# A hybrid layer: prompt attention, delta stages, memory keys and sample attention put together anew

## The reference, cut to what matters

```python
def gdn_chunked(q, k, v, g, beta, s0):          # per chunk of c rows and head
    gcum = cumsum(g)
    dec_strict, dec_incl = exp(gcum_i - gcum_j) for i > j, i >= j
    tmat = eye(c) + beta * dec_strict * (k @ k.T)
    w  = solve(tmat, beta * exp(gcum) * k)      # unit lower triangular
    uv = solve(tmat, beta * v)
    qk = (q @ k.T) * dec_incl
    u  = uv - w @ s
    o  = exp(gcum) * (q @ s) + qk @ u
    s  = exp(gcum_last) * s + (k * exp(gcum_last - gcum)).T @ u

def mem_kv(mem, g_mem, w_xk, w_xv, g_xk):
    mn = rmsnorm(mem, g_mem)
    return rmsnorm((mn @ w_xk) by heads, g_xk), mn @ w_xv
```

## Time and profile before

| | |
|---|---|
| median of three runs | 3438.41 us |
| profiled execution | 3432.61 us, span 3430.7 us |
| mean granted TensorE clock | 0.944 |
| prompt attention | 742.5 to 1129.1 us of the span |
| gate stage | 1129.1 to 1150.3 |
| prompt delta stage | 1150.3 to 1545.4 |
| sample delta stage | 1545.4 to 1653.8 |
| window attention of the sample | 1653.8 to 1771.0 |
| memory keys | 1771.0 to 1831.5 |
| output projection | from 1831.5 |

### The profile page before, as it was taken

One profiled execution on the slowest core, in us unless ns is written; L12 is line 12 of the kernel. 1 busy time (PEld: TensorE's weight loads), 2 busy tenths in 40 slices (PEclk: granted clock), 3 DMA queues, 4 the chain that ended last, 5 costly groups with the idle time before them and its releaser, 6 DMA issues. The chain is left out here.

```text
span 3430.7 us, 63305 instructions
## 1 busy us (share of the span) xinstructions
PE 3035.9 (88%) x22904; PEld 2636.5 (77%) x22949; DVE 1782.0 (52%) x2700; ACT 1472.6 (43%) x2924; POOL 411.2 (12%) x394
## 2 busy tenths in 40 slices
PE   7999999979999599975557999599749999999998
PEld 7999999978888488864335888488638888888886
DVE  5244055545554355553324776244377867676572
ACT  5112145435556365542122332255425655565552
POOL 1000000000000000000320000111112222222222
PEclk9999999989999799996688999799869999999999
DMA  5333433223335211111772433533349988989792
GB/s 170 115 107 129 162 110 116 92 86 124 123 127 170 75 36 57 64 47 45 241 245 81 137 126 111 183 115 136 124 168 325 323 291 295 330 300 320 227 316 55
DMA packets 299855, 549.18 MB, mean 160 GB/s; under 512 B 80675, under 2 KB 136879, under 8 KB 299130
## 3 DMA queue, kind: packets, MB, share of 16 engines
q1 hardware_dynamic: 261722, 406.68, 35.1%
q0 software_dynamic: 33712, 137.63, 12.8%
q10 hardware_dynamic: 4224, 2.10, 0.2%
HBM read 436.49 MB, written 143.39 MB: 169 GB/s over the span
## 5 line engine op out<-in xcount | busy, mean ns | idle before, releaser
L136 PE MATMUL pj_pu<-pj_w,pj_nT 128*128 128x256 f32 (+3 forms) x1088 | 307.2, 282 | 0.0
L137 PE MATMUL pj_pu<-pj_w,pj_nT 128*128 128x256 f32 (+3 forms) x1088 | 306.3, 282 | 0.0
L138 PE MATMUL pj_pu<-pj_w,pj_nT 128*128 128x256 f32 (+3 forms) x1088 | 305.6, 281 | 0.0
L137 PEld LDWEIGHTS pj_pu<-pj_w,pj_nT 128*128 128x128 f32 (+1 forms) x1088 | 202.5, 186 | 0.0
L138 PEld LDWEIGHTS pj_pu<-pj_w,pj_nT 128*128 128x128 f32 (+1 forms) x1088 | 202.4, 186 | 0.0
L136 PEld LDWEIGHTS pj_pu<-pj_w,pj_nT 128*128 128x128 f32 (+1 forms) x1088 | 202.0, 186 | 0.1
L3183 ACT ACTIVATE ex_gate<-xw_gate_raw 128x2048 fp32r<-128x2048 f32 x64 | 120.7, 1918 | 167.8 <-PE ex_gu L138 96.5
L716 ACT ACTIVATE att_prob<-att_score,att_res 128x256 f32<-128x256 f32 (+1 forms) x384 | 127.6, 443 | 142.6 <-DVE att_res L752 142.6
L3244 DVE TENSOR_TENSOR ex_down<-xw_down_raw,ex_down 128x2048 fp32r<-128x2048 f32 x64 | 146.6, 2291 | 79.7 <-ACT ex_down L3183 62.3
L136 PE MATMUL pj_pu<-pj_nT,pj_w 128*128 128x384 f32 (+2 forms) x480 | 175.3, 365 | 0.0
L758 DVE COPY att_pT<-att_turn 128x512 f32<-128x512 f32 (+1 forms) x192 | 107.3, 573 | 129.3 <-PE att_turn L812 128.8
(11 more groups left out here) (581 smaller groups left out, 7877.0 us busy)
## 6 DMA issues: line engine op xcount, KB each, us to landing
xw_gate_raw<-in_w_gate SPq DMA_DIRECT2D x64, 1024.0 KB, 6.9
xw_up_raw<-in_w_up SPq DMA_DIRECT2D x64, 1024.0 KB, 9.2
xw_down_raw<-in_w_down SPq DMA_DIRECT2D x64, 1024.0 KB, 11.2
out_win_k<-in_cache_k POOLq DMA_DIRECT2D x8, 2032.0 KB, 13.0
out_win_v<-in_cache_v POOLq DMA_DIRECT2D x8, 2032.0 KB, 13.7
tmp_att<-att_res POOLq DMA_DIRECT2D x48, 264.0 KB, 4.6
po_att<-tmp_att SPq DMA_DIRECT2D x16, 792.0 KB, 4.5
pj_raw<-in_w_in SPq DMA_DIRECT2D x24, 512.0 KB, 5.4
```

Of the source, the lines that this page charges most:

```text
L136: pe.matmul(out, ah, bh, start=start, stop=False)
L137: pe.matmul(out, ah, bl, start=False, stop=False)
L138: return pe.matmul(out, al, bh, start=False, stop=stop)
```

## The change

Prompt attention and prompt delta stage are put into one stage, "ag", which holds the attention's result ring, the gate inputs, six of the delta constants (the seventh, ident, comes with the gate inputs) and the ring of input tiles. SP issues the loads of all these behind its last attention load. POOL's wait for the attention stores moves to the end of delta_prompt's POOL program. The gate block has no SP program any more; the rows are stored and read back at the start of delta_prompt's main block, and PE waits for them only before the first tile's sums. As before, each DMA adds 16 to its semaphore.

The sample delta stage is a new function, delta_sample, in one block and with 64 rows (`C` = 64) throughout. The state's loads, four of 512 KB, z and one gain are issued on ACT's queue ahead of its first exponential. The state now is the weight (128x128), and 16 columns, eight rows of the turned W and of q of that sequence (`WQ`), move through it; the result is turned back by PE. The masked u is made by ACT, the eight products for the new state go through four banks, and the state is stored by SP in four pieces, two after each half. The memory rows, gains and the two weights for the memory keys are loaded by SP during this block.

memory_kv now follows at once, and during it SP loads queries, keys and values of the first sequence for the window attention, which comes next. The first rows for project_out lie in the tile `raw` of the weight split, and are loaded in the window attention's block, after POOL's splits are done and ahead of the stores of its results.

The diff, cut to its core (`-` lines of the old sample stage are left out):

```diff
+    with Stage(nc, "ag") as o:
+        res = o.sb("res", [P, 4, AH * (AD + 1) + AH])
...
+        def first_inputs(sp):
+            for dst, src in ((ab[:], t["zab"][0:PT, :, BW:].rearrange("n p c -> p n c")), (par[:], t["gate_par"]),
+                             (ss[:].rearrange("p a h n -> p (a h n)"), t["ss"]), (m[:], t["gp_sums"]), (ident[:], t["ident"])):
+                sp.dma_start(dst, src).then_inc(sems["loaded"], 16)
+            for dst, name in ((identb, "identb"), (eye, "gp_eye"), (sel, "gp_sel"), (maskb, "gp_mask"), (lvl, "gp_lvl"), (gout, "g_gdn")):
+                sp.dma_start(dst[:], t[name]).then_inc(sems["consts_in"], 16)
+            for n in range(3):
+                sp.dma_start(uu[:, n].rearrange("p a h d -> p (a h d)"), t["uu"][n]).then_inc(sems[f"u_in{n}"], 16)
+
+        attend_prompt(nc, t, res, att_stored, first_inputs)
+        delta_prompt(nc, t, (ab, ss, par, m, piece, ident), (identb, eye, sel, maskb, lvl, gout, uu), sems, att_stored)
...
+                ahead(sp)
...
-                for k in range(RES):
-                    pool.wait_ge(stored[k], NB // RES * 16)
...
+                sp.dma_start(ab[:].rearrange("p a h -> p (a h)"), t["zab"][PT, R, BW:]).then_inc(E["gates_in"], 16)
+                sp.dma_start(par[:], t["gate_par"][R]).then_inc(E["gates_in"], 16)
+                sp.dma_start(m[:], t["gs_sums"][R, :, R]).then_inc(E["gates_in"], 16)
+                sp.dma_start(uu[:].rearrange("p a h d -> p (a h d)"), t["uu"][PT, R]).then_inc(E["u_in"], 16)
+                for dst, name in ((ident, "ident"), (rm, "gs_rows"), (ones, "ones"), (identb, "identb"), (maskb, "gs_mask"), (lvl, "gs_lvl")):
+                    sp.dma_start(dst[:], t[name]).then_inc(E["consts_in"], 16)
+                if ahead:
+                    ahead(sp)
+                sp.wait_ge(E["pad_ok"], 1)
+                sp.wait_ge(E["ob_ok"], 1)
+                sp.dma_start(t["ob"][PT], ob[:].rearrange("p h d -> p (h d)")).then_inc(E["stored"], 16)
+                for a in range(2):
+                    sp.wait_ge(E["S_ok"], BH * a + BH)
+                    for b in (4 * a, 4 * a + 2):
+                        sp.dma_start(t["delta_s"][b:b + 2].rearrange("b h k v -> k (b h) v"),
+                                     S[:, b:b + 2].rearrange("p b h d -> p (b h) d")).then_inc(E["S_out"], 16)
+                sp.wait_ge(E["stored"], 16)
+                sp.wait_ge(E["S_out"], 64)
...
+                act.dma_start(z[:].rearrange("p h d -> p (h d)"), t["zab"][PT, R, 0:BW]).then_inc(E["z_in"], 16)
+                act.dma_start(gout[:], t["g_gdn"]).then_inc(E["z_in"], 16)
+                for b in range(0, B, 2):
+                    act.dma_start(S[:, b:b + 2].rearrange("p b h d -> p (b h) d"), t["delta0"][b:b + 2].rearrange("b h k v -> k (b h) v")).then_inc(E["S_in"], 16)
+                act.wait_ge(E["gates_in"], 48)
+                act.activation(na[:], par[:, 0], ACT.Exp).then_inc(E["na_ok"], 1)
+                act.wait_ge(E["ax_ok"], 1)
+                act.activation(ax[:], ax[:], ACT.Exp).then_inc(E["ln_ok"], 1)
...
+                for b in range(B):
+                    if b == 4:
+                        act.wait_ge(E["o_mm"], 1)
+                        act.activation(sqo[:], po, ACT.Square).then_inc(E["o_sq"], 1)
+                    act.activation(um[:, b], u[:], ACT.Copy, scale=rm[R, 0, b:b + 1]).then_inc(E["um_ok"], 1)
...
+                def decayed(b):
+                    V(S[:, b], S[:, b], bc(last[:, :, b], [P, BH, BD]), ALU.mult).then_inc(E["Sl_ok"], 1)
+
+                def grown_by(n):
+                    a, h = divmod(n, BH)
+                    dve.wait_ge(E["Sl_ok"], 4 * a + 4)
+                    dve.wait_ge(E["ds_mm"], n + 1)
+                    V(S[:, 4 * a:4 * a + 4, h, :], S[:, 4 * a:4 * a + 4, h, :], grown[n % 4], ALU.add).then_inc(E["S_ok"], 1)
...
+                pe.wait_ge(E["S_in"], 64)
+                pe.wait_ge(E["qgT_ok"], 1)
+                pe.wait_ge(E["WT_ok"], 1)
+                flat = pt[:].rearrange("p a h n -> p (a h n)").rearrange("p (h b k) -> p h b k", h=BH, b=B)
+                for h in range(BH):
+                    for b in range(B):
+                        mm = pe.matmul(flat[:, h, b, :], S[:, b, h, :], WQ[:, h, :, DEC_T * b:DEC_T * b + DEC_T], start=True, stop=True)
+                mm.then_inc(E["wq_mm"], 1)
...
+                for n in range(2 * BH):
+                    a, h = divmod(n, BH)
+                    pe.wait_ge(E["um_ok"], 4 * a + 4)
+                    need(pe, E["S_ok"], n - 3)
+                    pe.matmul(grown[n % 4], kt[:, h], um[:, 4 * a:4 * a + 4, h, :], start=True, stop=True).then_inc(E["ds_mm"], 1)
...
-            @block.sync
-            def _(sp):
-                for dst, src in ((ab[:], t["zab"][0:PT, :, BW:].rearrange("n p c -> p n c")), (par[:], t["gate_par"]),
-                                 (ss[:].rearrange("p a h n -> p (a h n)"), t["ss"]), (m[:], t["gp_sums"]), (ident[:], t["ident"])):
-                    sp.dma_start(dst, src).then_inc(loaded, 16)
-                sp.wait_ge(dv, 25)
-                sp.dma_start(t["b_rows"].rearrange("k p m t -> m (k p) t"), piece[:].rearrange("m k p t -> m (k p) t")).then_inc(kept, 16)
-                sp.wait_ge(kept, 16)
-                sp.dma_start(rw[:], t["b_rows"].rearrange("k p (h n) t -> (p h) k n t", h=BH)).then_inc(rows_in, 16)
-                sp.wait_ge(rows_in, 16)
...
-                rows(0)
-                for dst, name in ((ident, "ident"), (identb, "identb"), (eye, "gp_eye"), (sel, "gp_sel"), (maskb, "gp_mask"), (lvl, "gp_lvl"), (gout, "g_gdn")):
-                    sp.dma_start(dst[:], t[name]).then_inc(E["consts_in"], 16)
-                for n in range(1, PT):
+                sp.dma_start(t["b_rows"].rearrange("k p m t -> m (k p) t"), piece[:].rearrange("m k p t -> m (k p) t")).then_inc(E["kept"], 16)
+                sp.wait_ge(E["kept"], 16)
+                sp.dma_start(rw[:], t["b_rows"].rearrange("k p (h n) t -> (p h) k n t", h=BH)).then_inc(E["rows_in"], 16)
+                for n in range(3, PT):
...
+                for done in att_stored:
+                    pool.wait_ge(done, 12 * 16)
...
+                    if n == 0:
+                        pe.wait_ge(E["rows_in"], 16)
...
+                    if b or not first:
+                        values(b)
...
+        def first_sequence(sp):
+            sp.dma_start(q[0:NS], t["q"][PT, 0:NS]).then_inc(keyed["q_in"], 16)
+            for dst, cache, new, near, far in ((kk[:, 0], t["cache_k"][0], t["k"], "k_near0", "k_far0"), (vv[:, 0], t["cache_v"][0], t["v"], "v_in0", "v_in0")):
+                sp.dma_start(dst[:, 2:6, :], cache[W_BUF // 2:].rearrange("(j p) c -> p j c", p=P)).then_inc(keyed[near], 16)
+                sp.dma_start(dst[0:DEC_T, 6, :], new[PT, 0:DEC_T]).then_inc(keyed[near], 16)
+                for j in range(2):
+                    rows = cache[0:W_BUF // 2].rearrange("(j n r) c -> j n r c", j=2, r=16)[j, :, 0:DEC_T, :]
+                    sp.dma_start(dst[:, j, :], rows).then_inc(keyed[far], 16)
...
+            def mem_inputs(sp):
+                sp.dma_start(ident[:], t["ident"]).then_inc(keyed["consts_in"], 16)
+                for dst, src in ((x[:], t["mem"].rearrange("n p d -> p n d")), (gm[:], t["g_mem"]), (gk[:], t["g_xk"])):
+                    sp.dma_start(dst, src).then_inc(mem_in["loaded"], 16)
+                for n, name in enumerate(("w_xk", "w_xv")):
+                    sp.dma_start(w[:, n], t[name].rearrange("(k p) c -> p k c", p=P)).then_inc(mem_in["w_in"], 16)
+
+            delta_sample(nc, t, mem_inputs)
+            memory_kv(nc, t, (ident, x, w, gm, gk), mem_in, keyed["consts_in"], first_sequence)
...
+            att = raw[:, 0:3 * WA].rearrange("p (a n) -> p a n", a=3)
+            cat = raw[:, 3 * WA:3 * WA + D]
+            gq = raw[:, 3 * WA + D:3 * WA + D + XD]
+            eye = raw[:, 3 * WA + D + XD:3 * WA + D + XD + P]
...
+                sp.wait_ge(raw_free, len(loads))
+                for dst, name in ((eye, "ident"), (gq, "g_xq")):
+                    sp.dma_start(dst, t[name]).then_inc(consts_in, 16)
+                sp.dma_start(att, t["att"][:, 0].rearrange("a p c -> p a c")).then_inc(att_in, 16)
                 sp.dma_start(cat[:, AW:], t["ob"][0]).then_inc(ob_in, 16)
 
-            memory_kv(nc, t, first_rows)
-            project_out(nc, t, w, wq, (ident, gq, att, cat), sems)
+            attend_sample(nc, t, False, lambda pool, s: halves_ahead(pool, s, loads, (gx[:], t["g_xattn"]), raw_free), first_rows, (ident, q, kk, vv, keyed))
+            project_out(nc, t, w, wq, (eye, gq, att, cat), sems)
```

More of the change, by code:

```diff
@@ L651, in attend_prompt @@
         raw_in = s.sem("raw_in0", "raw_in1", "raw_in2")
-        stored = s.sem(*[f"stored{k}" for k in range(RES)])
         v_in = s.sem("v_in0", "v_in1", "v_in2", "v_in3")
@@ L1047, in delta_net @@
-        G = gates(nc, s, t, cst, tiles, first, 0 if sample else 2, pk, constants)
```

(38 more changed lines are left out.)

810 lines of the change are left out of this document (293 added, 517 removed).

## The result

The changed kernel takes 3379.07 us (median; 3378.79 to 3384.86) against 3438.41: a ratio of 0.9824, interval 0.9810 to 0.9837. It was forecast at 3357, and falls into the range; of the 81 us forecast, 59 came.

A forecast was written before the change was run, and what follows sets the result against it. PE, busy 88% of the span, loses time where it stands still, mostly in chains of waits. Terms 7.2+11.0-0.7+45+11.2+7+0.7 = 81.4 us off 3432.6 give 3351.2, as a median 3357; range 3337 to 3382.

The forecast's parts named there:

- rival A: Sample delta stage stays slow, PE at low clock and ACT issues at 1.35: gain 30 not 45, 3372 us; chance 0.22.
- rival B: Window stage gives nothing, DMA at 0.91 and added loads eating what is saved: 3364 us; chance 0.12.
- Part 1: End of prompt attention to gates: store wait removed, gate loads issued early, so DVE starts 7.2 us earlier.
- Part 2: Gates to first sums: constants and input tiles already loaded, only exit, store and reload left; 11.0 us less.
- Part 3: The stage holding the shared tiles has its own exit: 0.7 us more.
- Part 4: Sample delta stage, cut at five points: 108.4 us becomes 63.2, 45 us less.
- (a): Sample delta stage, start to transposes of the keys: one block, inputs loaded beside the gates; 22.7 to 17.0 us.
- (c): Sample delta stage, solve's first matmul to products with the state: half widths, two masked DVE copies gone; 13.8 to 6.9 us.
- (d): Sample delta stage, state products to first products for the new state: 64 weight loads at 8.3; 23.6 to 13.7 us.
- (e): Sample delta stage, new-state products to last addition's end: four banks, masks on ACT, PE and DVE overlap; 24.0 to 12.8 us.
- (f): Sample delta stage's tail: half the state stored early, two stores remain; 11.5 to 6.3 us.
- Part 6: Window attention: first sequence already loaded, second key load goes out earlier, fewer bytes; 7 us less, ends 0 and 12.

The follow-up runs named there:

- second profile: Changed kernel run again with no edit and profiled: median 3375.13 us, profile span 3373.8 us.
- first profile: Profile of the changed kernel as first measured, of its slowest execution: 3384.86 us, span 3383.2 us.

## Why the prediction was right, and where it was not

The direction, the order of the parts and the range held; the sum was 22 us too large by the medians. Half of that is one term. The range held because its slow end was set by rival A's time, plus 10: A and B, which the prediction priced one at a time, came together, and their 15 and 7 us make 3379. That this is the median to the microsecond is luck, since parts 1 to 3 and 5 fell short by 1 to 5 us each as well.

- **Part 4**, cut by cut, forecast and then measured (second profile): (a) 17.0, 16.3; (b) 6.5, 5.9; (c) 6.9, 11.5; (d) 13.7, 19.1; (e) 12.8, 14.8; (f) 6.3, 8.1. What failed in (d) is the clock: I took the state products at 8.3, near the full clock's 6.9, and they took 13.83, above the low-clock bound of 12.5 that I had worked out; that is the whole excess of (d), and with the clock up 36 of the 64 went at 0.103 each. Rows of the old stage speak for such a price, but for a reason that the change removes. Its two sets of state products (windows, columns as above):

```profile
1594.70:1603.30 8.60, 8.57 (x64) 8.60 (x65) 2.08 (x1) 0.00 (x0) 0.00 (x0) 0.80 0.00 0
1603.30:1610.50 7.20, 7.20 (x68) 7.03 (x66) 0.68 (x1) 0.00 (x0) 0.00 (x0) 1.00 0.01 2
```

  They had a PEclk of 0.80 and 1.00. But that clock had come up in the old stage's own work ahead of them, and the rewrite puts products half as wide in its place; the new stage is at 0.50 from its start to its end. No run separates what in the new work leaves the clock low. For (c) and (e) the low clock is argued: PE is busy for 9.0 of 11.6 us in (c) and nearly throughout (e), all at 0.50, and no run has either with the clock up. Estimate for (c): with these 9.0 halved it would take 7.1, near the forecast's 6.9. Rival A named this cause and the gain that it leaves, 30; measured 33. Its other half came too: the six issues on ACT took 8.0 us in the first profile and not 4.8, but only 3.5 to 4.4 of them lay on the path, so (a) held. What failed in (f) is the queue: I had half of the state stored early, but in SP's program these stores stand behind the wait for the output rows, and all four went out together. One sum was also wrong: the extremes named for (a), (d) and (e) give 35 to 50 us and not 38 to 52.
- **Part 6**: the outcome of rival B, and not its reason. The transfer that was moved was not hidden before, yet the stage kept its length; at 118.2 us in the first profile it met the prediction's own sign of being wrong, a window stage no shorter than 117. The loads put in did not eat what was saved: two megabytes fewer (32.7 by 117.2 us at 279 GB/s, 30.5 by 118.2 at 258) ran at a lower rate. Closing the hole and doubling the buffer did not help, taking out another 1.5 MB seems to. Why the same engines, as busy as before, move 266 GB/s at a share of 0.95 where they moved 279 at 0.91, stays open, and with it the cause of this miss.
- **Part 3**: the give-back that was not forecast. Part 2 brought the sums forward, and PE then stood still from its copies to the reload (3.6 us in the second profile) just before them, so the first 11 to 16 us from the sums on ran at 0.50; before, the clock was 0.97 over the first 2.5 us of them. I had asked whether the transposes fit under the reload, not what the wait leaves to the clock. The added exit, forecast at 0.7, took 0.3.
- **Part 1**: the wait and the loads went, at the size forecast, 2.3 and 5.2 us. What failed is the step that the early loads hinder nothing of the attention's: its last store lands beside them, 3.1 and 1.2 us later than before, and the drain ends that much later.
- **Part 2**: the store of the rows came back after 3.84 and 3.52 us where I kept the old 2.43, and the reload took 3.4 and 3.2 to the sums where I had 2.9. The exit, 0.87, was right.
- **Part 5** came as worked out at its start (first projection after 6.5 us, forecast 6.7).
- Rival C did not come: the state was there in time. E did not either: from some 70 us into project_out on PEclk is 0.93 and then 0.97 in both programs.

## What to carry to other kernels

When a stage is rewritten, don't carry the clock of its old rows over: ask which of the work that ran ahead of a product is still there, and price the product at both levels. Here that was 5.5 us on one group of products. Ask of every early issue which instruction of the issuing engine stands behind it: six DMA issues on ACT, and a wait ahead of two stores on SP, cost 4 and 2 us here. Ask also which last transfer it runs beside: 14 early loads made the attention's last store land 1.2 to 3.1 us later, with a barrier waiting for it. And where POOL's own store stands last before a barrier, its drain is on the path; issuing the last stores from SP took 5.2 to 7.2 us off it.

## What the runs showed of the hardware

POOL's drain took 3.98 us behind a wait for its store's landing; without that wait it took 5.4 to 7.4 us and ended 1.9 to 2.0 us after the landing in each of nine profiles. A store of 264 KB landed 2.3 us after its issue at a DMA share of 0.35, and 3.4 to 5.4 with other loads in flight at 0.99 and 1.00. TensorE's granted clock rose to 1.00 in a run of 384-column products; it was 0.50 through the 33 us of mostly narrower ones that followed in one kernel, though PE is recorded busy; and of 64 products of 16 columns behind such a run the first 3.7 us had 1.00, the next 4 us 0.63.
